# The compressed branch of a sparse-attention block, run in pieces between the attention units

## The reference

```
blocks = kv[:, idx] + pos_emb          # 31 blocks of 32 tokens, stride 16
hid = gelu(blocks_flat @ w1)           # 2048 -> 256, for keys and for values
kc, vc = hid @ w2                      # 256 -> 64; kc is rotated
p_cmp = masked_softmax(q @ kc.T)       # 512 x 31, 8 heads
o_cmp = p_cmp @ vc
out = g0 * o_cmp + g1 * o_slc + g2 * o_win
```

## Time and profile before

| | |
|---|---|
| median of 3 runs | 2844.16 us |
| the profiled execution | 2845.36 us, span 2843.6 us |
| PE busy / DVE / ACT / POOL, share of span | 96% / 53% / 38% / 7% |
| mean granted TensorE clock, share of 2.4 GHz | 0.972 |
| loads of `w_ada`, 512 KB each, median to landing | 4.2 us |

### The profile page before, as it was taken

One profiled execution on the slowest core, in us unless ns is written; L12 is line 12 of the kernel. 1 busy time (PEld: TensorE's weight loads), 2 busy tenths in 40 slices (PEclk: granted clock), 3 DMA queues, 4 the chain that ended last, 5 costly groups with the idle time before them and its releaser, 6 DMA issues.

```text
span 2843.6 us, 33322 instructions
## 1 busy us (share of the span) xinstructions
PE 2720.2 (96%) x13009; PEld 2261.9 (80%) x13009; DVE 1506.6 (53%) x2472; ACT 1078.4 (38%) x1464; POOL 199.7 (7%) x127
## 2 busy tenths in 40 slices
PE   7977998999999997799999999999999999999997
PEld 6866776888787886688888888888888888888886
DVE  4364554555534664467767656565424444444444
ACT  4342453433325434433333345555433333333332
POOL 0020000000000000000011233333100000000000
PEclk9986999999999999899999999999999999999999
DMA  5321442233232321233444535454666566556552
GB/s 175 92 90 52 119 132 76 89 95 96 89 97 77 94 75 37 94 96 104 141 131 147 156 119 221 161 219 159 230 213 213 186 204 201 186 187 206 192 185 82
DMA packets 142364, 392.11 MB, mean 138 GB/s; under 512 B 10944, under 2 KB 44752, under 8 KB 140688
## 3 DMA queue, kind: packets, MB, share of 16 engines
q1 hardware_dynamic: 88032, 274.86, 30.5%
q10 hardware_dynamic: 51904, 102.77, 10.3%
q0 software_dynamic: 2288, 12.54, 1.2%
HBM read 318.82 MB, written 71.30 MB: 137 GB/s over the span
## 4 chain that ended last, share of the span: by engine, by line
PE 93%; DVE 3%; ACT 2%; DMA 1%; issue 0%; DVEq 0%; POOL 0%; ACTq 0%; SPq 0%; POOLq 0%
PE PS L263 27%; PE PS L264 27%; PE PS L265 27%; PE PS L1871 4%; PE PS L1709 2%; PE PS L1751 1%; PE PS L1788 1%; PE PS L1740 1%; PE PS L1712 1%; PE PS L1849 1%; PE PS L1687 0%; DMA RAW<-in_w_in 0%; PE PS L407 0%; PE PS L413 0%; DMA A<-in_subk 0%
## 5 line engine op out<-in xcount | busy, mean ns | idle before, releaser
L258 DVE TENSOR_TENSOR WL<-RAW,WH 128x1024 fp32r<-128x1024 f32 x462 | 593.4, 1287 | 807.8 <-ACT WH L252 761.4
L263 PE MATMUL PS<-HH,WH 128*128 128x512 f32 x1696 | 668.4, 394 | 12.9 <-DMA A<-in_subk 7.2
L252 ACT ACTIVATE WH<-RAW 128x1024 fp32r<-128x1024 f32 x462 | 486.1, 1053 | 469.3 <-PE PS L265 447.7
L264 PE MATMUL PS<-HL,WH 128*128 128x512 f32 x1696 | 661.2, 390 | 0.0
L265 PE MATMUL PS<-HH,WL 128*128 128x512 f32 x1696 | 661.1, 390 | 0.0
L263 PE MATMUL PS<-WH,WGH 128*128 128x512 f32 x1024 | 398.5, 389 | 0.7 <-ACT ROW L990 0.7
L264 PE MATMUL PS<-WL,WGH 128*128 128x512 f32 x1024 | 398.3, 389 | 0.0
L265 PE MATMUL PS<-WH,WGL 128*128 128x512 f32 x1024 | 398.3, 389 | 0.0
L263 PEld LDWEIGHTS PS<-HH,WH 128*128 128x128 f32 x1696 | 319.4, 188 | 80.2 <-DMA A<-in_subk 7.5
L265 PEld LDWEIGHTS PS<-HH,WL 128*128 128x128 f32 x1696 | 318.9, 188 | 66.7
L264 PEld LDWEIGHTS PS<-HL,WH 128*128 128x128 f32 x1696 | 319.3, 188 | 63.2
(11 more groups left out here) (318 smaller groups left out, 2963.6 us busy)
## 6 DMA issues: line engine op xcount, KB each, us to landing
RAW<-in_peer_u SPq DMA_DIRECT2D x128, 512.0 KB, 3.7
RAW<-in_peer_v SPq DMA_DIRECT2D x128, 512.0 KB, 4.2
gate_matrices<-A ACTq DMA_DIRECT2D x8, 4096.0 KB, 12.4
A<-gate_matrices ACTq DMA_DIRECT2D x32, 1024.0 KB, 7.5
A<-acts ACTq DMA_DIRECT2D x32, 1024.0 KB, 10.7
RAW<-in_w_ada SPq DMA_DIRECT2D x48, 512.0 KB, 4.2
RAW<-in_ffn_up SPq DMA_DIRECT2D x44, 512.0 KB, 3.6
acts<-GATE SPq DMA_DIRECT2D x64, 256.0 KB, 2.6
```

The source lines that it names most:

```text
L252: nc.scalar.activation(WHr[:, slot(c), 0:w], RAW[:, slot(c), 0:w], ACT.Copy).then_inc(sem("high_done"), 1)
L258: nc.vector.tensor_tensor(WLr[:, slot(c), 0:w], RAW[:, slot(c), 0:w], WH[:, slot(c), 0:w], ALU.subtract).then_inc(sem("low_done"), 1)
L263: nc.tensor.matmul(out, L[0], R[0], start=first, stop=False)
L264: nc.tensor.matmul(out, L[0], R[1], start=False, stop=False)
```

## The change

The three barriers "projection", "compression" and "compressed attention" are gone. What stood between them is moved:

- POOL issues its three loads at once, and copies the compressed branch's keys and values as soon as the fifth block of the projection is stored. PE turns them while ACT stores the sixth. ACT then stores them, before the eight retention heads. POOL builds the blocks during retention, in the half of `Y` that the attention writes later; ACT and DVE split them there.
- ACT's gates, silu, mask copies and a preload of the square-root table move up beside retention. DVE's normalisation of retention loses the wait behind each instruction (`link`).
- The loop over units begins as soon as heads, masks and normalisation are there. Steps 0 to 3 hold two chunks of `cmp_w1` each (bank 6), and from step 4 groups of five steps hold four chunks of `w_ada` each (bank 7), now half as wide in columns and twice as deep in rows; the twelve half-sums are copied, turned and added in the fifth step (`summed_at`).
- Gelu stands at step 5, the turns and the second layer at 6 to 11, the scores at 12, 13, 15 and 16, the softmax at 14 and 17 to 21, the turns of the probabilities at 23 and 25, the outputs at 27, 29, 31, 33, and their gated additions at 28, 30, 32, 34. The selected branch writes `Y` first and the compressed one is added.

More of the change, by code:

```diff
@@ L815, in _ @@
                                  ACT.Sqrt).then_inc(sem("gn_root"), 1)
[L816 to L840, removed]
+            store_heads(range(12, 20))
             for s in range(len(units) + 1):
+                g = summed_at(s)
+                if g is not None and (g // 2) % 3 < 2:
+                    act.wait_ge(sem("chunk_used"), FIRST["ada"] + 4 * (g + 1))
+                    nc.scalar.activation(MODROW, PS[:, 7, :], ACT.Copy).then_inc(sem("mod_row"), 1)
                 if s < len(units):
@@ L1198, in _ @@
-            link(last)
-            barrier(dve, "compressed attention")
+            E4f = E4.rearrange("p t h n -> p (t h) n")
             for s in range(len(units) + 2):
@@ L1696, in _ @@
-            last.then_inc(sem("cmp_pt"), 1)
-            pe.wait_ge(sem("cmp_pt_stored"), 1)
-            for t in range(NT):
-                for g in range(2):
-                    last = nc.tensor.matmul(PS[:, t, 256 * g:256 * g + 256], PTC[:, 2 * t + g, :],
-                                            VBD[:, g].rearrange("p r n -> p (r n)"), start=True, stop=True)
-            last.then_inc(sem("cmp_out"), 1)
-            barrier(pe, "compressed attention")
-            pe.wait_ge(sem("ca_low"), 1)
+            turn_heads(range(8, 20))
@@ L1730, in _ @@
+                g = summed_at(s)
+                if g is not None and (g // 2) % 3 < 2:
+                    pe.wait_ge(sem("mod_row"), g - 2 * (g // 6) + 1)
+                    for n in range(4):
+                        last = nc.tensor.matmul(PS[:, 7, n:n + 1], MODROW[:, n * P:(n + 1) * P], ident[:, 0:1],
                                                 start=True, stop=True)
                     last.then_inc(sem("mod_turned"), 1)
+                if s == 6:
+                    pe.wait_ge(sem("hid_gelu"), 1)
+                    for w in range(2):
+                        for f in range(2):
+                            last = nc.tensor.transpose(PS[:, 6, P * w + 64 * f:P * w + 64 * f + 64],
+                                                       HT[0:64, w, f * P:(f + 1) * P], ident[0:64, 0:64])
+                    last.then_inc(sem("hid_turned"), 1)
@@ new lines, in _ @@
+                if s == 8:
+                    pe.wait_ge(sem("hid_stored"), 1)
+                    for f in range(2):
+                        nc.tensor.matmul(PS[0:64, 6, 256:320], HIDK[:, f, :], W2[:, 0, f, :], start=(f == 0), stop=(f == 1))
+                    for g in range(2):
+                        for f in range(2):
+                            last = nc.tensor.matmul(PS[:, 6, 320 + 64 * g:384 + 64 * g], HID[:, f, g].rearrange("p r n -> p (r n)"),
+                                                    W2[:, 1, f, :], start=(f == 0), stop=(f == 1))
+                    last.then_inc(sem("kc_ready"), 1)
@@ new lines, in _ @@
+                if s in (23, 25):
+                    n = (s - 23) // 2
+                    pe.wait_ge(sem("cmp_probs"), 1)
+                    wait(pe, "cmp_pt_stored", n)
+                    for u in range(4):
+                        t, g = 2 * n + u // 2, u % 2
+                        last = nc.tensor.transpose(PS[:, 6, u * P:(u + 1) * P],
+                                                   E4[:, t, 4 * g:4 * g + 4, :].rearrange("p h n -> p (h n)"), ident)
+                    last.then_inc(sem("cmp_pt"), 1)
@@ L1732, in _ @@
+                if s in (27, 29, 31, 33):
+                    t = (s - 27) // 2
+                    pe.wait_ge(sem("cmp_pt_stored"), 2)
+                    wait(pe, "cmp_added", t)
+                    for g in range(2):
+                        last = nc.tensor.matmul(PS[:, 6, 256 * g:256 * g + 256], PTC[:, 2 * t + g, :],
+                                                VBD[:, g].rearrange("p r n -> p (r n)"), start=True, stop=True)
+                    last.then_inc(sem("cmp_out"), 1)
                 u = s - 1
```

399 lines of the change are left out of this document (201 added, 198 removed).

## The result

The changed kernel takes 2829.36 us (median of 5 runs, 2819.14 to 2833.1) against 2844.16: ratio 0.9941, 95% interval 0.993 to 0.9953. That is 14.8 us faster where 41.6 were forecast, and 6 us outside the range. The profiled execution took 2819.14 us with a span of 2817.4, so 26.2 us less than the span before. It is compared first; why the median lies 10 us above it comes later.

A forecast was written before the change was run, and what follows sets the result against it. PE, busy 96% of the span, bounds the kernel; time returns only from idling or low clock. Chunks 66.6 us earlier, 25.4 more loop work and 0.4 less loop loss give -41.6 us: 2803 us, range 2784 to 2823.

The forecast's parts named there:

- Head start at the projection's barrier: Before retention: removing the barrier, where PE sat idle 3.0 us, gives 1 us, bounds -2 and +2.
- POOL's blocks: Beside retention: POOL's 12.3 us of block building and the splits fit beside 19 us of retention, with DVE mostly free.
- The start, 183.7: First compression chunk of the loop begins at 183.7 us, bounds 181 to 187, making the loop's chunks 66.6 us earlier.
- Normalisation, 0.30 a scaling: Between retention and first chunk: 16 scalings at 0.30 us, bounds 0.22 and 0.44, plus three gatings, 7.1 us.
- The clock at the loop's start: Loop's first steps: clock costs 1.5 us, against up to 8.25 if transposes don't count as PE-busy.
- What the loop takes in: PE work moved into the loop: first layer, scores, outputs, turns, second layer; 25.4 us at full clock, bounds 24 and 36.
- Waits: PE's waits in the loop: 1.1 us steps 0-6, 2.8 steps 18-23, 1.5 steps 28-35, 5.2 for row copies.
- The clock, 1.5 + 2.5 + 9.9 = 13.9 us: Loop's clock loss: 1.5 us at the start, 2.5 in steps 18-23, 9.9 at three turns or the narrow scores.
- The range: Whole kernel: 2784 to 2823 us; the sum's own range was 2793 to 2813.
- Rival D: First chunk waits for normalisation, heads and splits; start slips from 183.7 towards 190 us: 2809; chance 5%.
- "wrong if" list: Signs of failure: loop under 225 us, DVE ending most PE waits, clock at 0.50 over many steps, chunk after 187.
- rival B: Loop's first half: DVE's queue becomes the bound, loss grows by some 20 us, gain 21: 2823; chance 15%.

The follow-up runs named there:

- pool_waits: Changed kernel with one added wait, so that POOL builds the blocks only after DVE's fourth rotation: median 2821.3 us.
- spread: Changed kernel with the softmax one piece a step on DVE and the scores in eight bursts instead of four, later pieces shifted: median 2831.9 us.
- pool_row: Changed kernel with POOL's blocks held until after the fourth rotation and the row copy put ahead of the weight split: median 2818.0 us.

## Why the prediction was wrong, step by step

- *Head start at the projection's barrier, 1 us.* Right: retention's first matmul began at 151.50 against 153.25, 1.75 earlier.
- *POOL's blocks "lie beside 19 us of retention, where DVE has most of its time free".* This step failed, and with it the silent one that retention keeps its length: 28.65 us instead of 18.8, which is the whole slip of 9.0 us at the first chunk. POOL's blocks lie in the first place beside DVE's last rotation, and cost it; holding POOL back took 4.9 us off retention and brought the chunk to 186.7 (shown). I had asked whether DVE has time, not whether the two engines can work at once.
- *The start, 183.7.* Even with POOL held it is 186.7. The blocks' and the condition's low parts, 2.4 + 1.2 us, now go ahead of the statistics on DVE, but hold them up by 0.8 us only. The other 4.9 us are retention at a granted clock of 0.50 where it had 1.00 before; the sum had a clock term for the loop and none for this stage. An earlier start than forecast (by 1.9 us there) hides part of it. Why the clock is low there stays open.
- *Normalisation, 0.30 a scaling.* Slightly too low for a scaling (0.33 to 0.34), slightly too high in sum: 6.5 us from the reciprocal's end to the chunk against 7.1, as only two gatings, of 0.68 and not 0.78, lie ahead of the chunk.
- *The clock at the loop's start, 1.5 us and not 8.25.* Right in this profile: PE was granted 0.56 and 0.59 from 188 to 192 us, with little but head turns to do, and 1.00 from 192 on. So the row was borne out against the rule of the Trainium skill ("TensorE: Matmul & The Clock Gate", Part 4) that transposes don't count. It is no constant: in `pool_waits` the loop began at 0.50 and stayed there until 192 us, 5 us after its first chunk.
- *What the loop takes in, 25.4 us.* Right within what the clock's decimals allow: the content rose from 188.4 to 216.6 by the first profile and 213.5 by the second, 25.1 to 28.2.
- *Waits.* 1.1 + 2.8 + 1.5 + 5.2 = 10.6 were forecast for the loop; PE idled 248.0 - 236.5 = 11.5 with the attention barrier in it, and in the loop's own 244.3 us (to 437.0) 8.3. Too high, the row copy above all. The loads of `w_ada`, costed at nothing, took none: 3.8 us to landing, 4.2 before.
- *The clock, 1.5 + 2.5 + 9.9 = 13.9 us.* Mis-sized: 19.8 in the profile, and 33.5 in that of the other group, to which seven of eleven executions belong. This term is the second that failed. I priced falls as single events of 3.3 us with the one profile of before as the measure, and gave +-7; the loss of the same kernel moves by more than that between executions (13.7 us between two).
- *The range.* From 2803.8, 9.0 us for the start, 6.2 for the loop and 0.2 behind it give the profiled 2819.2; 10 us for the group give the median. Rival D had the start's slip, with the chance 5% and 190 as its end; together with dearer clock falls it left the range. No rival joined two.

Of the "wrong if" list two came true: the chunk began after 187, and DVE ended most of PE's waits in the loop (5.7 of 8.7 us). The second did not mean what it was written for: rival B expected some 20 us of them.

## What to carry to other kernels

Before work on GpSimd is moved, look at which VectorE operations it will run beside and where their inputs are: two inputs in SBUF cost more than double beside it, one in PSUM nothing here. Ask of every stage that the change touches, and not only of the one it rewrites, at which clock it will run. A sequence that hands over early (here a copy one step sooner) can be worth several times the wait in view: 7.9 us of loop for 2.5 us, with the clock's loss going down as well. But gains of this kind didn't add up when joined. When a forecast leans on the clock, take two or three profiles of one kernel before pricing a fall, give the range at least their spread, and compare kernels group by group, not by medians that a few executions in the other group can move by 10 us.

## What the runs showed of the hardware

- One kernel, same instructions, two groups of executions some 11 us apart (means 2820.6 and 2831.8). Between one profile of each, 9.9 us lie in the loop, from the granted clock alone (0.71 against 0.57 from 240 to 280 us). `spread`'s eleven lie from 2818.7 to 2839.9.
- TensorE's idling cost about twice its own length: 26 to 28 us of median for 14 to 15 us more idling, before the one-column turns.
- A VectorE operation on 128x64 elements with both inputs in SBUF went from 0.22 to 0.74 us beside GpSimd's 0.74 us additions; a 128x512 one with an input in PSUM took 0.69 us with and without.
- TensorE was granted 0.50 in retention from 156 to 164 us around 5.7 us of idling, and still 0.50 from 152 to 162 us with that idling gone (`pool_waits`), where the kernel before had 1.00: taking the long idle away did not bring the clock back.
- What stays open: why the clock is low in retention's first half even with POOL held, which event starts the long fall between steps 8 and 17, which came with narrow and with wide scores, and whether an earlier start brings a lower clock, as `pool_row` suggests. Only this is shown: the time of one kernel varies with the clock, and it fell by more than the waits that were taken away and rose by more than the idling that was added.
